# FF2 of the second layer by block transposes through HBM, with one pair of row chunks by seven products

## What is computed

```python
def conv_gated_ffn(h, w_up, conv_w, conv_b, w_down):
    u = h @ w_up                                     # 256 x 2048 by 2048 x 11264
    up_ = jnp.pad(u, ((0, 0), (1, 1), (0, 0)))       # three taps along the tokens
    u = up_[:, :-2] * conv_w[0] + up_[:, 1:-1] * conv_w[1] + up_[:, 2:] * conv_w[2] + conv_b
    gate, val = jnp.split(u, 2, axis=-1)
    return (jax.nn.silu(gate) * val) @ w_down
```

## Time and profile before

| | us |
|---|---|
| median of 3 runs | 2127.88 |
| their range | 2124.9 to 2128.0 |
| the profiled execution | 2125.52 |
| its span, first to last instruction | 2123.4 |

### The profile page before, as it was taken

The page is one execution under the profiler, slowest core; times in us unless marked ns, Lnnn a source line. Parts: engine busy times, 40 slices in busy tenths (PEclk is TensorE's granted clock), DMA queues, the critical chain, the costliest instruction groups (busy, mean ns, idle before and its releaser), DMA issues.

```text
span 2123.4 us, 28090 instructions
## 1 busy us (share of the span) xinstructions
PE 2108.5 (99%) x9682; PEld 1753.0 (83%) x9682; DVE 1738.8 (82%) x2498; ACT 1194.7 (56%) x1562; POOL 80.4 (4%) x114
## 2 busy tenths in 40 slices
PE   9999999999999999999999999999999999999999
PEld 7897888888888888888889878888888888888887
DVE  5889977888888887979766557569999999999787
ACT  6556675555555545545466446556666666665454
POOL 1000000001000100000000042000000000000000
PEclk9999999999999999999999999999999999999999
DMA  7665355677767767566556544466666666656665
GB/s 225 197 181 169 111 181 155 214 231 231 224 208 227 237 213 242 191 215 199 173 164 173 169 115 152 148 184 187 194 191 185 199 188 194 190 184 199 210 198 178
DMA packets 219710, 404.81 MB, mean 191 GB/s; under 512 B 14335, under 2 KB 58953, under 8 KB 219371
## 3 DMA queue, kind: packets, MB, share of 16 engines
q1 hardware_dynamic: 215755, 391.13, 59.5%
q0 software_dynamic: 3696, 11.54, 1.7%
q10 hardware_dynamic: 176, 1.06, 0.1%
HBM read 395.80 MB, written 7.86 MB: 190 GB/s over the span
## 4 chain that ended last, share of the span: by engine, by line
PE 82%; DVE 11%; issue 4%; ACT 2%; DMA 0%; DVEq 0%; ACTq 0%; POOL 0%; POOLq 0%
PE ps L679 20%; PE ps L681 20%; PE ps L680 20%; PE ps L985 6%; PE ps L986 6%; PE ps L987 6%; DVE w_lo L2075 3%; DVE gate_T L2128 2%; DVE val_T L2128 1%; PE ps L717 1%; ACT w_hi L1398 1%; DVE stage L2941 1%; DVE stage L2949 1%; DVE cv L2187 1%; PE ps L741 0%
## 5 line engine op out<-in xcount | busy, mean ns | idle before, releaser
L2075 DVE TENSOR_TENSOR w_lo<-raw,w_hi 128x1024 fp32r<-128x1024 f32 (+2 forms) x701 | 837.7, 1209 | 210.5 <-ACT w_hi L1398 204.0
L1398 ACT ACTIVATE w_hi<-raw 128x1024 fp32r<-128x1024 f32 (+2 forms) x701 | 724.6, 1045 | 459.2 <-PE ps L681 348.3
L679 PE MATMUL ps<-w_hi,hT_hi 128*128 128x512 f32 (+2 forms) x1792 | 699.8, 390 | 3.0 <-DVE w_lo L2075 2.3
L681 PE MATMUL ps<-w_hi,hT_lo 128*128 128x512 f32 (+2 forms) x1792 | 690.6, 385 | 0.0
L680 PE MATMUL ps<-w_lo,hT_hi 128*128 128x512 f32 (+2 forms) x1792 | 690.3, 385 | 0.0
L679 PEld LDWEIGHTS ps<-w_hi,hT_hi 128*128 128x128 f32 x1792 | 336.6, 188 | 72.7 <-DVE w_lo L2075 6.9
L681 PEld LDWEIGHTS ps<-w_hi,hT_lo 128*128 128x128 f32 x1792 | 336.4, 188 | 63.2
L680 PEld LDWEIGHTS ps<-w_lo,hT_hi 128*128 128x128 f32 x1792 | 336.8, 188 | 59.8
L679 PE MATMUL ps<-w_hi,aT_hi 128*128 128x512 f32 x480 | 187.1, 390 | 0.8 <-DVE w_lo L2075 0.8
L681 PE MATMUL ps<-w_hi,aT_lo 128*128 128x512 f32 x480 | 186.8, 389 | 0.0
L680 PE MATMUL ps<-w_lo,aT_hi 128*128 128x512 f32 x480 | 186.7, 389 | 0.0
(11 more groups left out here) (391 smaller groups left out, 2324.0 us busy)
## 6 DMA issues: line engine op xcount, KB each, us to landing
raw<-in_w_up SPq DMA_DIRECT2D x264, 512.0 KB, 4.2
raw<-in_w_down SPq DMA_DIRECT2D x176, 512.0 KB, 4.7
raw<-in_w_gate SPq DMA_DIRECT2D x88, 512.0 KB, 3.8
raw<-in_w_in SPq DMA_DIRECT2D x80, 464.0 KB, 3.7
raw<-in_w_out SPq DMA_DIRECT2D x64, 512.0 KB, 4.0
raw<-in_w_in SPq DMA_DIRECT2D x64, 256.0 KB, 3.2
raw<-in_w_in SPq DMA_DIRECT2D x24, 448.0 KB, 3.5
turn_rows<-stage POOLq DMA_DIRECT2D x11, 512.0 KB, 5.0
```

The costliest lines, as they stand in the source:

```text
L679: pe.matmul(o, xh, wh, start=first, stop=False)
L681: mm = pe.matmul(o, xl, wh, start=False, stop=last)
L1398: act.activation(w_hi[:, s, :kc, :width], raw[:, s, :kc, :width], ACT.Copy).then_inc(hi_ready, 1)
L2075: dve.tensor_tensor(w_lo[:, s, :kc, :width], raw[:, s, :kc, :width], w_hi[:, s, :kc, :width].bitcast(F32), ALU.subtract).then_inc(lo_ready, 1)
```

## The change

In each of FF2's turns 1 to 10 one pair of row chunks (tiles 7 and 8) is multiplied by seven products, `up_seven`: 21 matmuls for 24. To hold all of a turn's work in 8 banks, the gate half ends inside the unit and is complete only when `up_extra` has added the extra banks; the value half is complete after the turn's last tile and `up_value_add` in the next turn. `copy2` waits for these adds. The strip transposes are replaced by `up_blocks` (two block transposes for a half), a store to HBM and four loads back by POOL (`up_strips`), and a reordering copy on ACT (`strips2`). The gate's copy goes to a place of its own (`gate_rows`) and is transposed at the start of the next turn, where the product and residue of the turn before that now stand as well (`product2(j - 2)`, `hidden_hi`, `hidden_lo`). The gate's conv stands behind the unit, the value's conv at the turn's last tiles. The combinations lie where `x_sb` was, so POOL stores `x_sb` (2 MB) to HBM ahead of turn 1 and loads it back after turn 10. In all groups of DN1 and DN2, `sums` moves behind the `lo` of its tile. `prod_T`, `by_strip` and the semaphores of FF1's unit are reused.

```diff
+UP_ORDER = [(0, i) for i in range(8)] + [(1, 7)] + [(1, i) for i in range(7)]
+UP_UNIT = 7
+UNITS1 = len(FF1_UNIT) * (FB - 1)
...
+        up_comb_hi, up_comb = overlay([("up_comb_hi", [P, 4, NB], F32R), ("up_comb", [P, 4, NB], F32)])
+        up_comb_lo = overlay([("under_up_comb", [P, 4, NB], F32), ("up_comb_lo", [P, 4, NB], F32R)])[1]
...
-                load_block(T_FF2, 16 * j, w_up2, [2] * 8, cols(j))
-                load_block(T_FF2 + 8, 16 * j, w_up2, [2] * 8, cols(j + FB))
+                for n, (half, i) in enumerate(UP_ORDER):
+                    load(T_FF2 + n, 16 * j, [w_up2, w_up2[:, :, DFF:]][half], 2 * i, cols(j))
...
+                if name == "x3":
+                    pool.dma_start(x_rows, x_sb[:].rearrange("p t n -> p (t n)")).then_inc(x_saved, 16)
+                    def up_strips(j, half, again):
+                        pool.wait_ge(turned, FB + 2 * j - 1 + half)
+                        pool.sem_inc(pool_seen)
+                        pool.dma_start(turn_rows[half], turn_out).then_inc(turn_saved, 16)
+                        pool.wait_ge(turn_saved, 16 * (FB + 2 * j - 1 + half))
+                        pool.sem_inc(pool_seen)
+                        if again and half == 0:
+                            pool.wait_ge(aT_ready, j - 1)
+                            pool.sem_inc(pool_seen)
+                        strips_back(half, stage[:, 1 + half].rearrange("p c s -> p (c s)"))
+                    up_strips(1, 0, False)
+                    up_strips(1, 1, False)
+                    with pool.Fori(2, FB + 1) as j:
+                        up_strips(j, 0, True)
+                        up_strips(j, 1, True)
+                    pool.wait_ge(ff_value, 2 * (FB - 1))
+                    pool.dma_start(x_sb[:].rearrange("p t n -> p (t n)"), x_rows).then_inc(x_back, 16)
...
+                c, k0 = T_FF2 + UP_UNIT, 2 * UP_ORDER[UP_UNIT][1]
+                a11, a12, a22 = ([h[:, k0 + k, t * P:(t + 1) * P] for h in H] for k, t in ((0, 0), (1, 0), (1, 1)))
+                b11, b21 = ([w[:, c % RING, k, :] for w in (w_hi, w_lo)] for k in range(2))
+                b22 = [w[:, (c + 1) % RING, 1, :] for w in (w_hi, w_lo)]
+                sums = [[up_s_hi[:, i, :], up_s_lo[:, i, :]] for i in range(4)]
+                comb = [[up_comb_hi[:, i, :], up_comb_lo[:, i, :]] for i in range(4)]
+                pe.wait_ge(lo_ready, c + 1 + 16 * j)
+                three(ps[:, 4, :], a11, b11, True, True)
+                three(ps[:, 0, :], a12, b21, False, True).then_inc(tile_used, 1)
+                pe.wait_ge(gemm_free[1], G_FF2 + j)
+                pe.wait_ge(lo_ready, c + 2 + 16 * j)
+                three(ps[:, 2, :], sums[3], b22, True, False).then_inc(tile_used, 1)
+                pe.wait_ge(ff_split, 2 * UNITS1 + 2 * j - 1)
+                three(ps[:, 7, :], sums[0], comb[0], True, True)
+                three(ps[:, 6, :], sums[1], comb[1], True, True).then_inc(ff_used, 1)
+                pe.wait_ge(ff_split, 2 * UNITS1 + 2 * j)
+                three(ps[:, 5, :], sums[2], comb[2], True, True)
+                three(ps[:, 1, :], a22, comb[3], False, True).then_inc(ff_used, 1)
...
-                ff_tiles(T_FF2, 16 * j, 0, 0, 8)
-                pe.wait_ge(gemm_free[1], G_FF2 + j)
-                ff_tiles(T_FF2 + 8, 16 * j, 1, 0, 8)
+                for n in range(UP_UNIT):
+                    gemm_tile(T_FF2 + n, 16 * j, H, 2 * n, pair(0), n == 0, False)
+                up_seven(j)
+                for n in range(UP_UNIT + 2, 16):
+                    up_value_tile(n, j)
...
+            def strips2(j, half):
+                act.wait_ge(turn_back, 64 * (FB + 2 * j + 1 + half))
+                act.activation(by_strip(half_T[:].rearrange("p c s -> p (c s)")),
+                               stage[:, 1 + half].rearrange("p c s -> p (c s)").rearrange("p (i m a) -> p i m a", i=4, a=32),
+                               ACT.Copy).then_inc(value_turned if half else gate_turned, 1)
...
+            def up_unit_hi(j):
+                c = T_FF2 + UP_UNIT + 1
+                act.wait_ge(raw_landed[c % RING], landed(c, 16 * j))
+                act.wait_ge(tile_used, c - RING + 1 + 16 * j)
+                act.activation(w_hi[:, c % RING, 1, :], raw[:, c % RING, 1, :], ACT.Copy).then_inc(hi_ready, 1)
+                for i in range(2):
+                    act.wait_ge(ff_ready, 2 * UNITS1 + 2 * j - 1 + i)
+                    act.activation(up_comb_hi[:, 2 * i:2 * i + 2, :], up_comb[:, 2 * i:2 * i + 2, :], ACT.Copy).then_inc(ff_hi, 1)
+            def up_turn(j, after):
+                hi_tiles(T_FF2, 16 * j, 0, 2)
+                if after:
+                    hidden_hi(j - 2)
+                hi_tiles(T_FF2, 16 * j, 2, 4)
+                copy2(j - 1, 1, after)
+                hi_tiles(T_FF2, 16 * j, 4, 8)
+                up_unit_hi(j)
+                hi_tiles(T_FF2, 16 * j, 9, 10)
+                strips2(j - 1, 0)
+                center2(j - 1, 0)
+                hi_tiles(T_FF2, 16 * j, 10, 12)
+                act.wait_ge(ff_used, 2 * UNITS1 + 2 * j)
+                act.activation(up_comb[:, 0, :], ps[:, 4, :], ACT.Copy).then_inc(ff_copied, 1)
+                silu2(j - 1)
+                hi_tiles(T_FF2, 16 * j, 12, 14)
+                copy2(j, 0, True)
+                strips2(j - 1, 1)
+                center2(j - 1, 1)
+                hi_tiles(T_FF2, 16 * j, 14, 16)
...
-                    if b == 0 and (q, p) in SUM_AT:
-                        sums(SUM_AT[q, p])
                     if b == 0 and p in SEVEN[q]:
                         combine(q, p)
                     if b == 1 and p in SEVEN[q]:
                         second_chunk_lo(c)
                     else:
                         split_lo(c, 0)
+                    if b == 0 and (q, p) in SUM_AT:
+                        sums(SUM_AT[q, p])
...
+            def up_blocks(half):
+                for t in range(TOK):
+                    out = turn_out.rearrange("p (q c t a) -> p t c q a", q=4, c=4, t=TOK)[:, t]
+                    ins = dve.transpose(out, up_rows[half][:, t, :].rearrange("p (c q b) -> p c q b", c=4, q=4))
+                ins.then_inc(turned, 1)
...
+            def up_combine(j):
+                c = T_FF2 + UP_UNIT
+                sa, sb_ = c % RING, (c + 1) % RING
+                dve.wait_ge(raw_landed[sa], landed(c, 16 * j))
+                dve.wait_ge(raw_landed[sb_], landed(c + 1, 16 * j))
+                t1, t3, t2, t4 = (up_comb[:, i, :] for i in range(4))
+                dve.tensor_tensor(t1, raw[:, sb_, 0, :], raw[:, sa, 0, :], ALU.subtract)
+                dve.tensor_tensor(t3, raw[:, sb_, 1, :], raw[:, sb_, 0, :], ALU.subtract).then_inc(ff_ready, 1)
+                dve.wait_ge(ff_ready, 2 * UNITS1 + 2 * j - 1)
+                dve.tensor_tensor(t2, raw[:, sb_, 1, :], t1, ALU.subtract).then_inc(ff_step, 1)
+                dve.wait_ge(ff_step, 4 * (FB - 1) + 3 * j - 2)
+                dve.tensor_tensor(t4, raw[:, sa, 1, :], t2, ALU.subtract).then_inc(ff_ready, 1)
+            def up_combine_rest(j):
+                c = T_FF2 + UP_UNIT + 1
+                dve.wait_ge(hi_ready, c + 1 + 16 * j)
+                dve.tensor_tensor(w_lo[:, c % RING, 1, :], raw[:, c % RING, 1, :], w_hi[:, c % RING, 1, :].bitcast(F32),
+                                  ALU.subtract).then_inc(lo_ready, 1)
+                for i in range(2):
+                    dve.wait_ge(ff_hi, 2 * UNITS1 + 2 * j - 1 + i)
+                    dve.tensor_tensor(up_comb_lo[:, 2 * i:2 * i + 2, :], up_comb[:, 2 * i:2 * i + 2, :],
+                                      up_comb_hi[:, 2 * i:2 * i + 2, :].bitcast(F32), ALU.subtract).then_inc(ff_split, 1)
+            def up_extra(j, part):
+                u1, u2, u3, u4 = (up_comb[:, i, :] for i in range(4))
+                if part == 0:
+                    dve.wait_ge(ff_copied, FB - 1 + j)
+                    dve.tensor_tensor(u2, ps[:, 5, :], u1, ALU.add).then_inc(ff_step, 1)
+                    dve.tensor_tensor(ps[:, 0, :], ps[:, 0, :], u1, ALU.add)
+                    dve.wait_ge(ff_step, 4 * (FB - 1) + 3 * j - 1)
+                    dve.tensor_tensor(u4, ps[:, 7, :], u2, ALU.add)
+                    dve.tensor_tensor(u3, ps[:, 6, :], u2, ALU.add).then_inc(ff_step, 1)
+                else:
+                    dve.wait_ge(ff_step, 4 * (FB - 1) + 3 * j)
+                    dve.tensor_tensor(u2, ps[:, 7, :], u3, ALU.add)
+                    dve.tensor_tensor(ps[:, 1, :], ps[:, 1, :], u3, ALU.add).then_inc(ff_added, 1)
+            def up_value_add(j):
+                dve.wait_ge(tile_used, T_FF2 + 16 + 16 * j)
+                dve.wait_ge(ff_added, FB - 1 + j)
+                dve.tensor_tensor(ps[:, 2, :], ps[:, 2, :], up_comb[:, 3, :], ALU.add)
+                dve.tensor_tensor(ps[:, 3, :], ps[:, 3, :], up_comb[:, 1, :], ALU.add).then_inc(ff_value, 1)
+                dve.wait_ge(ff_value, FB - 1 + j)
...
+            def up_turn(j, after):
```

(65 more changed lines are left out.)

127 lines of the change are left out of this document (74 added, 53 removed).

## The result

The changed kernel takes 2158.5 us (median of 4 runs, 2156.0 to 2164.8) against 2127.9: a ratio of 1.0152, 95% interval 1.0128 to 1.0175, or 30.6 us more. The forecast was 2143.0, so 15.1 more. The sign was right; the size was half of what came.

The account below looks back on a forecast made before the run. DVE's queue was taken to bound FF2: 38.8 + 4.2 + 1.1 + 0.7 = 44.8 us a turn against 43.75. FF2's +8.1 and DN2's +7 on 2127.88 gave 2143.0 us, range 2126 to 2164.

Parts of the forecast that it names:

- DVE as the bound: FF2's loop: DVE's queue with its detours over ACT sets the pace, 44.8 us a turn against 43.75; chance 0.6.
- PE share near 95%: FF2's loop: a sign that the forecast is right, PE's busy share falling to near 95%.
- DVE's load: FF2's turn: DVE's work without waits falls from 42.2 to 38.8 us.
- Wait (a): FF2's turn: DVE stands for tile 14's `hi`, queued on ACT behind the gate's `copy2`, 4.2 us with handoffs.
- Wait (b): FF2's turn: DVE stands for tile 4's `hi`, queued on ACT behind the value's `copy2`, 1.1 us.
- Wait (c): FF2's turn: DVE stands at `up_combine` for tile 8's load, 0.3 to 1.4 us, taken as 0.7.
- FF2's sum: FF2's loop: turn 1 -0.9, turn 2 +0.6, eight turns of +1.05, together +8.1 us (+4.9 to +14).
- DN2's start: Start of DN2 after turn 10: new PE waits, less those of before, net +7 us (+3 to +10).
- the walk: Start of DN2: queues followed step by step, giving PE waits of 1.6, 1.9, 2.6 and, in later pairs, 2.6 us.
- Sums: DN groups: `sums` behind the `lo` brings that `lo` 1.8 us earlier; PE hardly waits there, so 0 to 1 gained.
- The return through HBM: FF2's turn: 12.5 us from the transposes' end to the last load back, covered by 1.4 us for the gate.
- third rival: FF2's loop: the loads back become last, ACT waits for DMA ahead of `strips2`; at 16 us, 2162 us; chance 0.2.

Follow-up runs that it names:

- the held return: The changed kernel with the gate's four loads back held until three of the four combinations are formed, in turns 2 to 10: 2189.4 us.
- the reordered version: The changed kernel with ACT's `hi` of tiles 4, 13, 14 and several copies reordered, also at DN2's start: 2119.6 us, ratio 0.9971 to the kernel before.

## Why the prediction was half right

*DVE as the bound*: right. PE follows in every turn, with the wait of about 2 us for tile 14's `lo` that was told (1.8 to 2.2 in turns 3 to 10), and moving ACT's instructions alone brings PE's pace back. "PE share near 95%" was 92% (43.76 of 47.36).

*DVE's load, 38.8*: 38.71 measured.

*Wait (a), 4.2*: 4.35, with the path that was named. *Wait (b), 1.1*: 0.93. Both were walked from rows of before.

*Wait (c), 0.7, bounds 0.3 to 1.4*: 2.44 in turns 3 to 10, 3.76 in turn 2. **This is the step that failed.** I bounded tile 8's landing by rows of before's FF2, in which POOL moves nothing, and took the low side "since this load mostly runs alone but beside a store". The prediction's own terms say otherwise. From the end of the gate's transposes to the end of tile 4's `lo` it is 4.9 us (value add 1.5, two `lo` 2.3, wait (b) 1.1), and to the first load back 5.9 (563.21 to 569.09): tile 8's load and the return start within 1 us of each other. I had both times and didn't lay them side by side. FF1 held a warning: its loads have a median of 4.6 us. With POOL's return and the value's store out of its way the wait is 0.40 (the held return), so the low end of the bounds would have been right.

*One small wait*, 0.23 us for ACT ahead of the residue (`hidden_lo`), wasn't in the sum.

*FF2's sum, +8.1*: +28.9 in the profile. Eight turns of 3.04 instead of 1.05 make 24.3 instead of 8.4, of which (c) has 13.9 (8 x 1.74) and the small wait 1.8. Turn 2, which I let off with 0.6 for PE's lead, cost 4.5: its (c) was 3.76, and less that it is 44.3 us, as long as a steady turn. Nothing was absorbed. Turns 0 and 1 came out even (+0.1) where I had -0.9.

*DN2's start, +7*: +8.1 for the whole of DN2, in part by other stalls than the walk had. PE waits 1.7 us at DN2's tile 11 (the walk had 1.9), 2.3 at tile 14 (2.6) and 1.6 in later pairs (2.6). It doesn't wait at tile 2, where the walk had 1.6, and does for 1.8 at tiles 8 and 9, where the walk had nothing. The clock is at full in all of DN2.

*Sums, 0 to 1 gained*: 3.4 to 4.6. I priced the `lo` that comes earlier only by PE's waits shown in before (0.76); DN2 of that kernel alone got 1.4 shorter, and where the rest of the medians' difference lies stays open.

*The return through HBM*: 12.5 us forecast. In the turn shown the gate's transposes begin at 1732.29, and the last load back, issued at 1739.7, has landed by 1746.1, 12.6 us after they end (1733.5). ACT comes to it at 1749.4. It was covered by 3.3 us instead of 1.4, since (c) holds ACT back as well. The held return shows the price of the third rival had it come. That 2158.5 lies beside this rival's 2162 is chance: its sign, ACT waiting for the DMA ahead of `strips2` in the loop, is nowhere in turns 2 to 10 (once, 4.4 us, in DN2's start). For the 512 KB store, "DMA: Bandwidth & Descriptors" of the Trainium skill would give the estimate of 3.2 us told in the prediction. The trace agrees with it for the gate's stores, which land after 3.1 to 3.4 us in turns 2 to 10, and not for the value's, which move beside the return and SP's loads and take 6.2 to 7.7. The median of 4.8 is that of neither.

*Profiled run and median*: of the 6.2 us between them the dip at 1092 us can hold about 3, if the other runs lack it. The mean clock doesn't set the profiled run apart (0.994, the others 0.993 to 0.995), and wait (c) alone scatters by 1.6 us from turn to turn; what made the difference stays open, since the other three runs left no trace.

## What to carry to other kernels

Before giving a load its lone price, write beside its issue what the other queues issue in the same 2 us; a median over a loop hides a few slow loads in sixteen, and the queue waits for just one of these. An engine with 4 us a turn to spare can still set the pace through detours over another engine, and these are cheap to remove: put what waits for a late result behind the next instruction that someone else waits for (36 us here for two moves in ACT's order). Price such a removal by the new bound, not by the wait's length.

## What the runs showed of the hardware

SP's load of 512 KB takes 3.2 to 3.6 us where nothing else is issued within 1.5 us of it (tiles 0 to 7 of turns 3 to 10). Issued within half a microsecond of the first of four loads of 128 KB by POOL it takes 5.6 in the mean, and the two loads behind it 7.1 and 7.3 (a mean of 8.6 in a variant).

The granted clock was at 1.2 instead of 2.4 GHz in stretches of 3.4 us (6.8 in some), mostly behind stalls of PE of some 2 us, but not behind each. In DN2 it fell behind stalls of 2.3 (the reordered version), 2.5 and 2.8 us and stayed at full behind one of 2.26 us of the changed kernel. The stall of 1.9 us at 208 us, which all profiles have, is followed by the lower clock in five of them. Near 1092 us it fell in five profiles with no wait of PE listed ahead of it, and nothing here tells why. In FF2 of the changed kernel it fell behind five of nine stalls of 1.8 to 2.2 us. The four in the midst of the loop cost nothing, for DVE set the pace: less its wait (c), a turn with it is no longer (44.3 to 44.4 us) than one without (44.4). In DN2 half the pace for 3.4 us is an estimated 1.7 us of lost work, part of which later waits gave back.

"Perfetto Trace Analysis" of the Trainium skill, on the most-contended engine, says to work first on the engine of highest occupancy, and to judge TensorE's headroom by its weight loads. Here PE went from 99% to 98% busy, its weight loads from 83% to 81% and DVE from 82% to 79%, while the time rose by 1.5%. Both engines got less work and the kernel got slower, so in these runs occupancy alone doesn't show the bound of a queue that waits on another; DVE's waits do.
